# A mixture-of-experts step: first weight set loaded without a copy and further ahead, token lists from one summed position, last tile routed from unnormed rows

## The reference, cut to what matters

```python
x = x + concat(conv_module(h), pooling_mixer(h)) @ w_out          # the mixer, h = rmsnorm(x, g_mix)
h2 = rmsnorm(x, g_ffn)
g_logits = h2 @ w_rg + b_rg                                       # 4 groups
e_logits = (h2 @ w_re + b_re) of the group with the largest g_logit   # 8 experts of it
e_val, e_idx = top_k(e_logits, 2)
gate = softmax(e_val) * softmax(g_logits)[group]
x = x + sum over the two: gate * (silu(h2 @ w_gate[e]) * (h2 @ w_up[e])) @ w_down[e]   # 32 experts, 512 wide
x = x + sigmoid(rmsnorm(x, g_ple) @ w_ple_gate + b) * (p @ w_ple_proj)
return rmsnorm(x, g_final), new conv and pool states
```

## Time and profile before

| | |
|---|---|
| runs | 1148.82, 1154.58, 1154.23 us, median 1154.23 |
| the profiled execution | 1147.95 us |
| its span, first to last instruction | 1146.2 us |
| busy: PE, PEld, DVE, ACT, POOL | 1073.5 (94%), 613.9 (54%), 513.5 (45%), 510.0 (44%), 291.3 (25%) us |
| granted PE clock, mean | 0.972 |
| DMA | 300.32 MB, mean 262 GB/s |

### The profile page before, as it was taken

One profiled execution on the slowest core, in us unless ns is written; L12 is line 12 of the kernel. 1 busy time (PEld: TensorE's weight loads), 2 busy tenths in 40 slices (PEclk: granted clock), 3 DMA queues, 4 the chain that ended last, 5 costly groups with the idle time before them and its releaser, 6 DMA issues.

```text
span 1146.2 us, 17858 instructions
## 1 busy us (share of the span) xinstructions
PE 1073.5 (94%) x5269; PEld 613.9 (54%) x5270; DVE 513.5 (45%) x665; ACT 510.0 (44%) x690; POOL 291.3 (25%) x308
## 2 busy tenths in 40 slices
PE   5999996999999877999999999999999999979996
PEld 5899985877887532333333333333333333338884
DVE  6588999884332352123123213212311313357785
ACT  6354547663321254336345435535533625434332
POOL 2177775784000100011111111111111101013310
PEclk9999997999999788999999999999999999989998
DMA  8212932311242949999999999999999999966531
GB/s 267 65 56 71 284 102 74 117 42 69 74 153 89 347 146 395 397 363 343 397 396 362 396 397 358 397 398 392 364 396 397 364 396 399 402 240 209 192 133 41
DMA packets 149297, 300.32 MB, mean 262 GB/s; under 512 B 12032, under 2 KB 42784, under 8 KB 149259
## 3 DMA queue, kind: packets, MB, share of 16 engines
q1 hardware_dynamic: 134907, 264.69, 62.9%
q0 software_dynamic: 6512, 22.29, 5.5%
q10 hardware_dynamic: 7840, 12.85, 3.0%
HBM read 261.72 MB, written 38.06 MB: 262 GB/s over the span
## 4 chain that ended last, share of the span: by engine, by line
PE 55%; DMA 3%; issue 1%; ACT 1%; DVE 1%; SPq 1%; ACTq 0%; POOL 0%; DVEq 0%; POOLq 0%
PE ps_gate_up L2026 28%; PE ps_y L2039 14%; PE ps_gate L65 3%; PE ps_gate L63 3%; PE ps_gate L64 3%; PE ps_x L2013 2%; DMA raw_weights<-w_exp_up 2%; PE ps_h L2046 2%; DMA y_rows<-y_tile 1%; PE ps_h3t L2330 1%; SPq L90 1%; DMA mixer<-y_rows,out_rows 0%; ACT weights L106 0%; PE ps_gate L141 0%; DVEq L2112 0%
## 5 line engine op out<-in xcount | busy, mean ns | idle before, releaser
L2026 PE MATMUL ps_gate_up<-weights,x_turned 128*64 128x512 f32 x1568 | 351.0, 600 | 1.2 <-ACT x_turned L1917 0.7
L106 ACT COPY weights<-raw_weights 128x2048 f32 (+1 forms) x99 | 185.6, 1899 | 108.1 <-issue 49.2
L2026 PEld LDWEIGHTS ps_gate_up<-weights,x_turned 128*64 128x64 f32 x1568 | 109.7, 138 | 207.8 <-issue 206.9
L106 DVE COPY weights<-raw_weights 128x2048 f32 x93 | 114.2, 1229 | 217.9 <-PE ps_gate_up L2026 74.6
L2039 PE MATMUL ps_y<-weights,h_turned 128*64 128x512 f32 x784 | 179.0, 598 | 0.9 <-ACT h_turned L1944 0.9
L447 POOL TENSOR_TENSOR conv_pool_taps<-conv_pool_taps,tap_product 128x448 f32<-128x448 f32 (+1 forms) x88 | 136.0, 1545 | 39.5 <-ACT tap_product L548 29.3
L115 POOL COPY token_ids<-item_tokens 128x1 int32 (+1 forms) x48 | 8.8, 183 | 445.2 <-PE ps_x L2013 445.2
L1983 DVE TENSOR_TENSOR hidden<-ps_gate_up,act_gate 128x256 f32<-128x256 f32 x49 | 20.8, 425 | 224.2 <-ACT act_gate L1935 216.0
L887 DVE SCALAR_TENSOR_TENSOR taps_bank<-a_ext,par,taps_bank 128x640 f32<-128x640 f32 (+1 forms) x128 | 101.5, 793 | 3.3
L2039 PEld LDWEIGHTS ps_y<-weights,h_turned 128*64 128x64 f32 x784 | 52.2, 136 | 93.3 <-issue 92.2
L548 ACT ACTIVATE tap_product<-a_ext,par 128x448 f32<-128x448 f32 (+1 forms) x104 | 75.4, 740 | 50.9 <-POOL conv_pool_taps L447 34.2
(11 more groups left out here) (282 smaller groups left out, 1551.8 us busy)
## 6 DMA issues: line engine op xcount, KB each, us to landing
raw_weights<-w_exp_gate SPq DMA_DIRECT2D x128, 512.0 KB
raw_weights<-w_exp_up SPq DMA_DIRECT2D x128, 512.0 KB
raw_weights<-w_exp_down SPq DMA_DIRECT2D x64, 1024.0 KB, 11.7
y_rows<-y_tile ACTq DMA_DIRECT2D x98, 128.0 KB, 5.4
y_rows<-zero_rows SPq DMA_DIRECT2D x16, 512.0 KB, 6.2
x_rows<-x_tile SPq DMA_DIRECT2D x9, 512.0 KB, 2.6
h_rows<-h_tile SPq DMA_DIRECT2D x9, 512.0 KB, 2.9
mixer<-x_rows SPq DMA_DIRECT2D x9, 512.0 KB, 4.6
```

The source lines that it names most:

```text
L106: copy(S.work[s][:, :], raw).then_inc(S.w_ready[s], 1)
L2026: last = pe.matmul(ps_gu[side[j], :, :], x_t[:, c, side[of]], w[:, :, share(D_EXP, j)], start=(k == 0), stop=(k == KD - 1))
```

## The change

It has five parts.

1. Set 0 is loaded straight into the working buffers S.work, which now lie beside S.raw from the start (piece_from), and ACT's six first copies go. The first three of its pieces are issued after the store of x2 of tile 8, the others after the store of h2 of tile 8, both in the mixer's stage. What was set 0's place in that stage, after tile 7, is now set 1's. Set 2's pieces 3 to 5 are asked for at the start of the routing stage and 0 to 2 at the start of the experts'. The order of experts has three fixed first places, not two. The waits in load_piece and copy_piece are moved by one set.
2. The mixer's stage no longer waits at its end for x2_stored[2] and h2_stored[0]; SP waits for the first in the routing stage before its first projection store, POOL for the second before the first gather.
3. Tile 8 is routed from x2 times gain (last_gain); its logits are multiplied by the row's rstd in the routing stage. Its transposes stand in the middle of the last out_products.
4. Routing: the index tables are made by POOL in the mixer's stage, between its powers of tiles 7 and 8. The start of an expert's blocks is added to the rank by PE in PSUM, so that one product and sum gives a row's slot; its block and its row come from it by rounding with a large constant. One-hot tables are bf16 with the row index last, so that the lists' matmuls read them with a stride. PE's projections are spread otherwise.
5. Behind the experts: the last y has a tile of its own; g_ple, b_ple and g_final rows are loaded in the middle of the experts' loop; x2 of tile 1 and projections of tiles 0 and 1 are loaded in the gate stage; late_project of the last tile is made whole ahead of the first transpose.

```diff
+def piece_from(eng, S, s, dst, e, loaded):
...
 def load_piece(eng, S, s, n, slot, e):
-    if type(n) is not int or n >= 1:
-        eng.wait_ge(S.raw_loaded[s], n * LANDED[s])
+    if type(n) is not int or n >= 2:
+        eng.wait_ge(S.raw_loaded[s], (n - 1) * LANDED[s])
...
-    if type(n) is not int or n >= 2:
+    if type(n) is not int or n >= 3:
         eng.wait_ge(S.w_ready[s], n - 1)
...
@@ front, sync @@
                     store(t)
+                    if t == TILES - 1:
+                        for s in PIECES[0:3]:
+                            piece_from(sp, S, s, S.work[s], slice(0, 1), S.first_loaded[s // DOWN[0]])
                     store_h(t)
+                    if t == TILES - 1:
+                        sp.wait_ge(x2_stored[0], 16 * (TILES // 3))
+                        for s in PIECES[3:]:
+                            piece_from(sp, S, s, S.work[s], slice(0, 1), S.first_loaded[s // DOWN[0]])
...
                         for s in PIECES:
-                            load_piece(sp, S, s, 0, 0, slice(0, 1))
-                for j in range(3):
+                            load_piece(sp, S, s, 1, 0, slice(1, 2))
+                for j in range(2):
                     sp.wait_ge(x2_stored[j], 16 * ((TILES + 2 - j) // 3))
-                for j in range(2):
-                    sp.wait_ge(h2_stored[j], 16 * ((TILES + 1 - j) // 2))
+                sp.wait_ge(h2_stored[1], 16 * (TILES // 2))
@@ front, gpsimd @@
                 rms_pow(7)
+                pool.wait_ge(out_ready, 2 * GROUP_TILES[4][0])
+                pool.wait_ge(x2_stored[0], 16 * (TILES // 3))
+                pool.wait_ge(h2_ready, TILES - 2)
+                routing_tables(pool, S)
                 rms_pow(8)
@@ front, scalar @@
-                square2(8)
                 h2t_leave(7, 1)
-                h2t_leave(8, 0)
-                h2t_leave(8, 1)
+                last_leave(0)
+                square2(8)
+                last_leave(1)
@@ front, vector @@
                 add(8, 0)
+                last_gain(0)
                 add(8, 1)
+                last_gain(1)
@@ front, tensor @@
-                out_products(8, 1)
+                out_products(8, 1, range(KH))
                 turn2(7, 1)
+                last_turn(0)
+                out_products(8, 1, range(KH, KD))
                 route(7)
-                turn2(8, 0)
-                turn2(8, 1)
-                route(8)
+                last_turn(1)
+                last_route(0)
+                last_route(1)
@@ routing, sync @@
                 for s in (3, 4, 5):
-                    load_piece(sp, S, s, 1, 1, slice(1, 2))
+                    load_piece(sp, S, s, 2, 1, slice(2, 3))
+                sp.wait_ge(S.x2_stored[2], 16 * (T // 3))
@@ routing, tensor @@
-                project(1)
-                pe.wait_ge(made, 6)
+                project(1, 0)
                 pe.wait_ge(to_rank, 1)
                 count_tokens()
                 rank_tokens()
+                project(1, 1, (0,))
                 pe.wait_ge(to_rank, 2)
                 pe.matmul(ps_order, ...)
                 pe.wait_ge(to_rank, 3)
-                pe.matmul(ps_starts, block_rows[0:E, :], sums[0:E, :], start=True, stop=True).then_inc(ranked, 1)
+                pe.matmul(ps_rank[:, :, :], block_rows[0:E, :], tab.sums[0:E, 0:E].unsqueeze(1).to_broadcast([E, T, E]),
+                          start=False, stop=True).then_inc(ranked, 1)
+                pe.wait_ge(to_rank, 4)
+                pe.matmul(ps_ends, block_rows[0:E, :], tab.sums[0:E, E:], start=True, stop=True).then_inc(ranked, 1)
...
-                for t in range(2, 4):
-                    turn_p(t + 1)
-                    project(t)
-                turn_p(5)
+                project(1, 1, (1,))
+                turn_p(3)
+                project(2, 0)
+                project(2, 1)
                 pe.wait_ge(to_place, 1)
                 list_tokens(0)
                 pe.wait_ge(to_place, 2)
                 list_tokens(1).then_inc(placed, 1)
-                project(4)
+                turn_p(4)
+                project(3, 0)
                 pe.wait_ge(to_place, 3)
                 pe.matmul(flat_tot[:, 0:ITEMS + 1], owners[:, :], ...)
-                for t in range(6, T):
-                    turn_p(t)
+                turn_p(5)
+                project(3, 1)
+                turn_p(6)
+                project(4, 0)
+                turn_p(7)
+                project(4, 1)
+                turn_p(8)
@@ routing, list_tokens @@
-                            last = pe.matmul(ps_items[h * BLOCK:(h + 1) * BLOCK, :], row_parts[j][:, a, :], at_item[:, a, :],
+                            last = pe.matmul(ps_items[h * BLOCK:(h + 1) * BLOCK, :], row_parts[j][:, :, a], at_item[:, :, a],
@@ routing, vector @@
-                tt(t32[:, :, :, :], oh[:, :, :, :], bc(ps_rank[:, :, :].unsqueeze(1), shape), ALU.mult)
-                red(rk[:, :, :], t32[:, :, :, :], ALU.add)
...
+                tt(t32[:, :, :, :], oh[:, :, :].rearrange("p e (k t) -> p k t e", k=2), bc(ps_rank[:, :, :].unsqueeze(1), shape), ALU.mult)
+                red(slot[:, :], t32[:, :, :, :].rearrange("p k t e -> p (k t) e"), ALU.add)
+                ts(nearest[:, :], slot[:, :], 0.5 - BLOCK / 2, NEAREST, ALU.add, ALU.add)
+                stt(row[:, :], nearest[:, :], -NEAREST, slot[:, :], ALU.add, ALU.subtract)
...
@@ experts, sync @@
-                for t in range(2):
-                    sp.dma_start(S.x2_in[t], S.x2_rows[t * P:(t + 1) * P, :]).then_inc(S.x2_loaded[t], 16)
...
-                for rows, src in zip((S.b_ple_rows, S.g_final_rows), gains[1:]):
-                    sp.dma_start(rows[:, :], src.partition_broadcast(P)).then_inc(S.ple_rows_loaded, 16)
+                sp.wait_ge(S.x2_stored[2], 16 * (TILES // 3))
+                sp.dma_start(S.x2_in[0], S.x2_rows[0:P, :]).then_inc(S.x2_loaded[0], 16)
@@ experts, scalar @@
-                leave_y(end)
-                store_y(end)
+                leave_y(end, y_end)
+                store_y(end, y_end)
@@ embedding_gate @@
+                load_x2(1)
+                load_proj(0)
+                load_proj(1)
...
-                late_project(pe, S, LATE + 3, ps_g[1], (0,))
+                late_project(pe, S, LATE + 3, ps_g[1])
                 turn_h(0, 0)
-                late_project(pe, S, LATE + 3, ps_g[1], (1,))
                 turn_h(0, 1)
```

472 lines of the change are left out of this document (266 added, 206 removed).

## The result

The changed kernel took 1160.63 us (median of 6 runs, 1159.40 to 1161.87) where the kernel before, run beside it, took 1150.41 (6 runs, 1148.82 to 1154.58): a ratio of 1.0078, with a 95% interval of 1.0060 to 1.0097. It is 0.8% slower. Forecast was a gain of 8.2 us. The profiled execution took 1160.29 us, with a span of 1158.5, 12.3 us longer than before.

A forecast was written before the change was run, and what follows sets the result against it. The kernel was taken as TensorE-bound (94% busy), with gains only in the seams; 3.2 - 2.65 + 1 - 3.75 - 6 = -8.2 us took the profiled 1147.95 us to 1139.7 (1146.0 against the runs' median). Range 1136 to 1155.

The forecast's parts named there:

- What bounds the kernel: Whole kernel: TensorE bound, 94% busy; experts' matmuls untouched by the change, gains only in seams where PE stands idle.
- Front, +3.2: Mixer's end: SP, held at about 1,650 outstanding packets, issues ten more weight loads; routing starts at 394.7, 3.2 us later.
- Rival A: Mixer's end: SP isn't held, the stage ends at 386.7, all behind 8 us earlier, 1138 us; chance 0.16.
- Routing stage, -2.65: Routing: PE reaches the lists at 19.3 us, first transpose of x at 31.4 instead of 34.06, 2.65 us gained.
- Strided reads, +1: Routing's 72 list matmuls read operands at a 36-byte stride: between nothing and 6.8 us, taken as 1 us lost.
- Rival B: Strided reads cost 5 us, or PE's clock falls, or tile 1's rows are late: 3 to 5 us lost, 1151; chance 0.24.
- Rival C: Lists' strided weight loads not hidden beside matmuls: 20 us more, 1165; decides from 0.13 us a pair; chance 0.08.
- ACT's copies and the stores of projections, nothing: Routing: six ACT copies removed bring nothing; queued projection stores cost nothing but are the next thing late.
- Start of the experts, -3.75: Between items 0 and 1: set 1 already loaded, gap 3.55 us instead of 7.3, 3.75 us gained.
- Rival D: Experts' start: set 0 queues behind set 1, item 1 waits as before, the 3.75 us stay away, 1150; chance 0.05.
- Gain rows, nothing: Middle of experts: 1.5 MB, 3.7 us of loads, in a stage where PE waits for no weight, cost nothing.
- End, -6: Behind the experts: last y's store halves, gather starts earlier, first gate product near 1022 instead of 1028.17, 6 us gained.

The follow-up runs named there:

- experiment 3: Changed kernel, set 0's loads moved from ahead of the mixer's last store into the routing stage: four of ten 1156.39 us, all ten 1150.96 us.
- experiment 6: Kernel of experiment 5 with packed one-hot table, projection stores ahead of set 2's first four loads: store 0 1142.42 us, stores 0 and 1 1135.41 us.
- experiment 7: Strides removed or restored: changed kernel, both packed, 1154.31 us; early store 0, one-hot strided, 1141.83; the best kernel, one-hot strided, 1137.72, lists too, 1142.51.
- experiment 5: Changed kernel with gain rows moved, lists packed, set 0's ten loads in routing, ScalarE's gate-weight copies earlier: 1145.04 us; variants: one-hot packed 1145.67, projection 1 later 1144.96.
- experiment 1: Changed kernel with the gain-row loads issued 13 us earlier in the experts' loop, ahead of a set's down pieces: 1154.47 us, ratio 1.0025.
- experiment 4: Changed kernel with ScalarE's two gate-weight copies moved ahead, before the last y's copy-out and its store: 1157.06 us, ratio 1.0044.
- the edits together: Changed kernel with the four edits of experiment 5, and at 1145.7 also the one-hot table packed: 1145.67 us, ratio 0.9955.
- experiment 7's first kernel: Changed kernel with both the lists' operands and the one-hot table read without a stride: 1154.31 us, ratio 1.0032.
- the best kernel: Kernel of experiment 5 with packed one-hot table, stores of projections 0 and 1 ahead of set 2's first four loads: 1135.41 us, ratio 0.9860.

## Why the prediction was wrong, step by step

- **What bounds the kernel.** Right that only the seams could win; wrong in "the change touches none of these matmuls". It put 1.5 MB into a stage whose DMA engines already had hardly any time to spare: in the kernel before they moved 385 GB/s from 460 to 1000 us, at a DMA share of 1.02.
- **Front, +3.2.** Right, measured +3.5, and by its mechanism: with fewer loads ahead of the last store, the stage begins 4.4 and 9.5 us earlier (experiment 3). The size leans on the count of 1,650 packets, which gave 7 us where 4.4 were measured, so how near the 3.2 came owes something to luck. Rival A, that SP isn't held, is refuted. The prediction treated this as a small loss and didn't see that it was the largest reserve.
- **Routing stage, -2.65.** Wrong: measured, with the next term, +7.8. The step that failed is "PE ... gets to the lists at 19.3": it got there at 24.2 (419.12 - 394.95). I took PE's work at the prices of before, and PE had become the engine that the chain waits for: 2.6 us more in counts and ranks, whose operands are strided too and for which I had no term at all, and 0.9 to 1.5 us a piece on the projections behind them, at 1.2 GHz. With the one-hot table packed PE got there at 19.1 (experiment 6, 405.88 - 386.78), as forecast, so the plan of the stage was sound and the price of the reads was not. The steps won on VectorE were real and hidden. Of the 9.4 us between forecast and measurement 4.9 lie ahead of the lists, 2.4 in them, and 2.2 behind them, where projection 3's first half ran at the lower clock.
- **Strided reads, +1.** Mis-sized: 3.4 us for the lists alone; 8.6 us in the profiles and 7.1 in the medians for lists, one-hot table and the clock behind it (experiment 7). I chose the end that lay near the old duration "so that loads and matmuls overlap". The Trainium skill (Advanced Engine Details and Errata, SBUF Cachelines), whose penalty for accesses that each go to another line I weighed, gives no size for it. The trace agrees that there is one: 72 matmuls in 4.75 us against 1.36 with only the layout changed. Rival B named this mechanism ("5 us") beside a fall of the clock, at a quarter of the chance. Rival C's price per pair (0.13 us) wasn't reached: 0.066.
- **ACT's copies and the stores of projections, nothing.** Right here (item 0 wasn't late), and right about "the next thing late": once the stage began earlier, that wait ate 5 to 9 us (experiments 5 and 6).
- **Start of the experts, -3.75.** Right, -3.8. Rival D is refuted. It varies with the clock that PE has when it starts, from 24.4 to 28.3 us for two items.
- **Gain rows, nothing.** Wrong, +5.4. The argument "in a stage in which PE waits for no weight" read the result of a balance as a reserve: the cycle has room for most of it, but not at that place (4.3 of the 5.4 us came back in experiment 1, 1.15 did not).
- **End, -6.** Mis-sized, -1.0. The store's gain came as forecast (4.2 of 4.6). Left out was what stands beside the gather: VectorE's subtractions, which in the changed kernel fall on two of POOL's issues, not one (+2.8; experiment 4 gives 2.3 back), and PE's lower clock in the first products (+1.5). POOL's first issue of 1.79 us in the trace before (experiment 4) was there to be read against 0.94 for the next ones.

## What to carry to other kernels

- Layout is part of a matmul's price. Here the strided operands of the lists cost TensorE 3.4 us and saved VectorE 0.6 us on each of three writes, and the work behind the strided one-hot table paid in clock as well.
- "No engine waits here" says that a stage is balanced, not that it has room; look at the DMA share too. Put added transfers where the issuing engine waits for a buffer, and keep stores that gate other engines ahead of prefetches in the same queue.
- When a loss is removed, look what comes late next, and time the edits together. Here the edits together left the first two stores of projections in charge, and they held back 10 us (1145.7 against 1135.4) until they were moved as well.

## What the runs showed of the hardware that I had not expected

- TensorE's clock stayed at 2.4 GHz in a stretch in which PE was 3.52 of 5 us busy (packed) and fell to 1.2 GHz in one behind counts and ranks in which it was busy throughout (strided). The fall at that place came in each of the 11 profiles with a strided one-hot table and in none of the four in which the changed kernel's table was packed. The stride isn't the only way to it: the kernel before, without one, fell at 406, after waits of 1.25 and 1.44 us, and experiment 7's first kernel at 418, after waits of 1.09 and 0.73 us, while the best kernel had the same waits and stayed at 1.00. What of the strided reads brings it about is open.
- The stride's price depends on the operands. Worked out from the differences, one column of the one-hot table (stride 18 bytes) costs 1.1 to 1.4 ns more in counts and ranks (0.32 us over 288 columns, 0.38 over 288, 1.62 over 1152, the last partly at the lower clock), but one of the lists' (stride 36 bytes, weights and moving columns both) 0.37 ns (3.39 us over 72 x 129). Why the lists' columns are cheaper wasn't tested.
- A store issued behind a full queue is 14 to 15.5 us under way (395.2 to 409.7 in experiment 6), though the same stores land in 2.6 to 3.3 us in the kernel before. The queue's length in packets, which I put at 1,650, wasn't measured by itself.
